# Two changed positions in the gate projection of a two-block transformer kernel: what the first copy of a head pair waits for, and where the second strip's gather stands on VectorE

## The reference, cut to what matters

```python
q, i_in, f_fw, f_bw, z = jnp.split(h @ w_in, 5, axis=-1)
for d, g in enumerate((f_fw, f_bw)):
    log_f = jnp.logaddexp(jnp.log(lbd), jnp.log1p(-lbd) + jax.nn.log_sigmoid(gf))
    k = (1.0 - lbd) * jax.nn.sigmoid(-gf)
...
o_l, _ = _hgrn2_bidir(q_l, v_l, gates_l, ctx_states)
...
o = _rmsnorm(o, o_gain).reshape(B, L, D_INNER).astype(z.dtype)
return (o * jax.nn.silu(z)) @ w_out
```

## Time and profile before

| | us |
|---|---|
| median of the runs | 2627.55 (2625.5 to 2629.52, 3 runs) |
| the profiled execution's own time | 2627.0 |
| its span in the trace | 2625.2 |
| PE busy | 2517.3 (96%) |
| DVE busy | 1199.5 (46%) |
| ACT busy | 605.6 (23%) |
| POOL busy | 258.0 (10%) |
| mean granted TensorE clock | 0.988 of full |

### The profile page before, as it was taken

The page is one execution under the profiler, slowest core; times in us unless marked ns, Lnnn a source line. Parts: engine busy times, 40 slices in busy tenths (PEclk is TensorE's granted clock), DMA queues, the critical chain, the costliest instruction groups (busy, mean ns, idle before and its releaser), DMA issues.

```text
span 2625.2 us, 33413 instructions
## 1 busy us (share of the span) xinstructions
PE 2517.3 (96%) x13400; PEld 1965.0 (75%) x13400; DVE 1199.5 (46%) x2083; ACT 605.6 (23%) x1202; POOL 258.0 (10%) x194
## 2 busy tenths in 40 slices
PE   7999999999999898899999999999999999999999
PEld 3687888878878576666786444678886587889998
DVE  2267585685775712254226111146665014115961
ACT  3132223232322112133224110021111013112211
POOL 0011111121111010000000000101210000003410
PEclk9999999999999998999999999999999999999999
DMA  9453343333424042212430122322333232254662
GB/s 352 157 177 128 112 144 112 133 144 117 149 96 145 2 143 77 79 40 56 125 97 17 48 80 64 97 64 82 96 102 89 66 80 65 81 178 135 170 174 68
DMA packets 320031, 284.83 MB, mean 108 GB/s; under 512 B 27650, under 2 KB 298634, under 8 KB 319546
## 3 DMA queue, kind: packets, MB, share of 16 engines
q1 hardware_dynamic: 318170, 279.08, 34.3%
q0 software_dynamic: 1280, 4.20, 0.4%
q10 hardware_dynamic: 479, 0.13, 0.0%
HBM read 280.24 MB, written 3.15 MB: 108 GB/s over the span
## 4 chain that ended last, share of the span: by engine, by line
PE 79%; DVE 12%; issue 7%; ACT 2%; DVEq 0%; POOL 0%; ACTq 0%; POOLq 0%
PE ps L1358 11%; PE ps L1287 9%; PE ps L721 9%; PE ps L1437 4%; PE ps L1425 4%; PE ps L781 4%; PE ps L1325 3%; PE ps L1299 3%; PE ps L819 3%; PE ps L905 2%; PE ps L976 2%; PE ps L925 2%; DVE arena L2316 2%; PE ps L1131 2%; PE ps L484 2%
## 5 line engine op out<-in xcount | busy, mean ns | idle before, releaser
L1287 PE MATMUL ps<-hT,ring_mem 128*128 128x512 f32 (+1 forms) x768 | 250.3, 486 | 0.0
L1287 PEld LDWEIGHTS ps<-hT,ring_mem 128*128 128x128 f32 x768 | 145.9, 190 | 101.3 <-issue 91.4
L721 PE MATMUL ps<-hT,ring_mem 128*128 128x256 f32 x672 | 164.2, 388 | 24.1 <-ACT arena L1592 16.3
L721 PE MATMUL ps<-xT,ring_mem 128*128 128x256 f32 x672 | 162.0, 384 | 7.2 <-DVE ring_mem L2013 7.2
L721 PEld LDWEIGHTS ps<-hT,ring_mem 128*128 128x128 f32 x672 | 127.7, 193 | 47.4 <-ACT arena L1592 19.1
L2247 DVE TENSOR_TENSOR arena<-ps,arena 128x512 f32<-128x512 f32 (+1 forms) x48 | 26.8, 558 | 291.3 <-PE ps L1299 291.3
L721 PEld LDWEIGHTS ps<-xT,ring_mem 128*128 128x128 f32 x672 | 129.6, 194 | 27.9 <-DVE ring_mem L2013 7.9
L1358 PE MATMUL ps<-hT,arena 128*128 128x256 f32 (+1 forms) x704 | 132.6, 333 | 6.9 <-ACT hT L505 6.9
L1358 PE MATMUL ps<-arena 128*128 128x256 f32 (+1 forms) x704 | 130.1, 328 | 0.0
L819 PE MATMUL ps<-arena,K_c 128*128 128x128 f32 x896 | 120.0, 288 | 8.5 <-ACT K_c L1629 8.4
L819 PEld LDWEIGHTS ps<-arena,K_c 128*128 128x128 f32 x896 | 116.4, 194 | 15.3 <-ACT K_c L1629 10.7
(11 more groups left out here) (307 smaller groups left out, 4324.0 us busy)
## 6 DMA issues: line engine op xcount, KB each, us to landing
ring_mem<-in_w_mod_dram SPq DMA_DIRECT2D x24, 2048.0 KB, 7.7
ring_mem<-in_w_up_dram SPq DMA_DIRECT2D x88, 512.0 KB, 5.2
ring_mem<-in_hg_w_in_dram SPq DMA_DIRECT2D x40, 1024.0 KB, 5.2
ring_mem<-in_w_in_dram SPq DMA_DIRECT2D x30, 1024.0 KB, 5.4
ring_mem<-in_w_down_dram SPq DMA_DIRECT2D x16, 1408.0 KB, 7.1
ring_mem<-in_ada_w_dram SPq DMA_DIRECT2D x8, 2048.0 KB, 7.7
ring_mem<-in_mla_w_in_dram SPq DMA_DIRECT2D x9, 1024.0 KB, 5.3
ring_mem<-in_hg_w_out_dram SPq DMA_DIRECT2D x8, 1024.0 KB, 12.1
```

Source lines behind the costliest of these rows:

```text
L721: mm = PE.matmul(dst, left[:, k, :], right[:, k, :], start=k == 0, stop=k == 3)
L1287: mm = PE.matmul(ps[:, j, 0:n], wj[:, k, m * 128:m * 128 + 128], hT[:, k, c0:T], start=k == 0, stop=k == 7)
```

## The change

Two edits. On ScalarE the copy of product one of a turn's first strip no longer waits for `unpacked` and `moved`, only for `o_full`; the copy of product two of the first strip now waits for these two. On VectorE, after term 3 of the scan, the gather of the second strip (`j` = 1, with the sums for the third) comes ahead of the read-out, where it came behind it. Terms 1, 5 and 7, at which other gathers stand, have no read-out.

```diff
@@ -1585,8 +1585,6 @@
             act.wait_ge(one_full, nth(i, j))
             if j == 0:
                 act.wait_ge(o_full, raised(i * 2 - 2))
-                act.wait_ge(unpacked, i)
-                act.wait_ge(moved, i)
             else:
                 act.wait_ge(whole_ready, nth(i, j - 1))
             S.activation(P1_hg, ps[:, 0, 0:256], ACT.Copy).then_inc(one_kept, 1)
@@ -1597,6 +1595,9 @@
 
         def hg_two_scalar(act, i, j):
             act.wait_ge(two_full, nth(i, j))
+            if j == 0:
+                act.wait_ge(unpacked, i)
+                act.wait_ge(moved, i)
             if j == 2:
                 act.wait_ge(lv_full, i * 16 - 14)
             S.activation(hg_part(j, 0, 256), ps[:, 0, 0:256], ACT.Copy).then_inc(two_kept, 1)
@@ -2407,10 +2408,10 @@
                     if not first and term == 2:
                         for hd in range(2):
                             hg_root_vector(dve, i - 1, hd)
+                    if gates and term % 2:
+                        hg_gather_vector(dve, st, i + 1, term // 2)
                     if not first and term == 3:
                         hg_read_vector(dve, st, i - 1)
-                    if gates and term % 2:
-                        hg_gather_vector(dve, st, i + 1, term // 2)
                     if gates and term == 4:
                         hg_mods_vector(dve, i + 1, 0)
                         for m in range(2):
```

## The result

| | before | changed |
|---|---|---|
| median, us | 2628.51 (4 runs) | 2599.82 (2596.28 to 2602.53, 4 runs) |
| ratio | | 0.9892, 95% interval 0.988 to 0.9904 |
| span of the profiled execution | 2625.2 | 2597.6 |
| PE busy | 2517.3 | 2508.6 |

The account below looks back on a forecast made before the run. PE was taken as the bound, busy 96% of the span. Gains of 20.9 us at the turn heads and 6.0 from the VectorE reordering, 26.9 together, gave a median of 2600.6 us, range 2594 to 2611.

Parts of the forecast that it names:

- What ended the wait at the head: Turn's head: PE's 2.63 us wait for the copy at 1592 ends with `unpacked`, not with `o_full` or the product.
- What is late next there: Turn's head: scores of term 1 wait for ScalarE's keys, starting at 9.63 instead of 11.99; 0.7 us of new waiting remains.
- The added wait at 1602: ScalarE's copy at 1602, now at 9.4 us, waits for `unpacked`, due at 5.7: costs nothing, 3.7 us in hand.
- the collision at the unpacking: GpSimd's 2510 of strip 0 lands beside VectorE's 1948 and 1951: bounds 0 and 1.07 us, taken as 0.
- The clock: Turn heads: about 5.4 us (four times 1.35) of the gain is clock coming back, if shorter waits leave it high.
- Edit two: VectorE after term 3, turns 2 to 7: 1.0 us per turn, 6.0 in all; ends 4.8 and 11.1.
- The tie between 2063 and GpSimd: Read-out's 2062 (now 2063) and GpSimd's 2510 start within 0.1 us; PE keeps 0.8, 1.3 or 1.85 us a turn.
- Rival A: Read-out beside GpSimd's sum: the collision is free, 1.85 us a turn, 32 in all, 2595.5 us; chance 0.18.
- Rival B: Term 5: the clock falls at the new waits of nearly 2 us, giving 2606 to 2610 us; chance 0.17.
- C: An unseen chain takes back most of the gain: about 9 us remain, 2618 us; chance 0.07.
- D: Turn's head: 1592 could be waiting for `o_full` or the product; no change, 2627 us; chance 0.03.
- E: Slower: low clock after the new waits at terms 1 and 5 in every turn, thirteen falls, up to 2642 us; chance 0.02.

Follow-up runs that it names:

- The written-out loop: ScalarE's loop over turns 1 to 6 written out instead of a Fori loop, against the changed kernel: 2597.35 us, ratio 0.9883.
- the kernel with the held sum: GpSimd's first sum of strip 2 waits until the products of term 4 are done, against the changed kernel: 2595.72 us, ratio 0.988.
- a kernel whose wait was 0.05 us longer: GpSimd's first sum of strip 2 waits until the read-out is done, against the changed kernel: 2609.83 us, one run.

## Why the prediction was right, point by point

- **What ended the wait at the head.** `unpacked` was last, as read from ScalarE's idle time: with both waits at the copy the head is 14.8 at clock 1.00, with only `moved` kept 13.2, with neither 12.4.
- **What is late next there.** 1596 plus 5.91 us gave 9.63 for the scores of term 1; they start at 9.56 (323.49 - 313.93). Head forecast 12.5, 11.8 and 11.7; measured 12.41, 11.71 and 11.59. The sum of the heads was forecast at 20.9 and measured at 21.4. The written-out loop showed that it was ScalarE's chain: a table load less, and the wait is gone.
- **The added wait at 1602 and the collision at the unpacking** cost nothing. The collision came at its full 1.07 us and was covered, within the bounds given.
- **The clock.** The 5.4 us came back: no head is below 1.00. A fall in turn 7 costs more than the 1.35 of the others: without one that head is 14.55 us in the kernel with edit two alone, against 16.24. The forecast of turn 7 does not hang on this.
- **Edit two.** Named were the four things that happened: PE 2.8 us ahead after the gather, a new wait of nearly 2 (1.79), 1970 back at 1.22, 2063 longer. The size was forecast at 6.0 and measured at 5.1. The tie between 2063 and GpSimd was taken in the middle (1.0 us a turn). In turns 2 to 6 GpSimd was ahead every time, by 0.03 to 0.05 us, and 2063 paid 1.0; in turn 7 VectorE won, and the gain there was 1.6. PE's 0.8 at the scores of term 5 shrinks by 0.1 in the scores themselves, which take 2.05 us behind the wait instead of 1.95. Taking the middle was a choice and not a reading; the rows of 1969 spoke for the full price.
- **Rival A** (no collision) is what the kernel with the held sum does: 1.7 us a turn instead of 0.7. **Rival B** (the clock falls at the new wait) did not come in the trace of the changed kernel and did in one of a kernel whose wait was 0.05 us longer, for 1.64 us in each of five turns. Its chance of 0.17 was no formality: five such falls would have made about 2608 of the 2599.8. That they stayed away is not explained by anything in the prediction, and in so far it was luck. **C, D and E** did not come. The thirteen falls of E are too many by the prediction's own waits, which are five at term 1 and six at term 5.
- **A premise of B that does not hold.** The prediction puts the new wait between 1.72 us, which the clock survived, and 2.63. The same trace of the kernel before has waits of 1.16 and 1.50 us, 2.6 us from one to the next, after which the clock was at 0.50:

```profile
1096.82 1.10 PE L431 MATMUL ps<-arena,ones 128*128 128x256 f32 x4 [1.16 <-ACT arena L400]
1099.42 2.05 PE L431 MATMUL ps<-arena,ones 128*128 128x512 f32 x2 [1.50 <-ACT arena L400]
```

```profile
1099.42:1101.42 2.00, 2.00 (x3) 0.97 (x4) 1.96 (x3) 0.00 (x0) 0.00 (x0) 0.50 0.00 0
```

So 1.72 us was no safe length.

- **Small misreadings.** The wait at the head of turn 2 was 2.46 us and not as long as the others. The part from line 484 on is 88.9 us in turns 2 to 7 and 85.9 in turn 1. Neither changes the sum.
- **How close it came** is partly chance. Over the turns the forecast was 26.9 and the measurement 26.5, with the heads 0.5 better and edit two 0.9 worse; another 1.0 us came from the part behind the turns, where nothing was changed.

## What to carry to other kernels

When a wait on several semaphores is split, look at which of them the engine's idle time names, and then follow the queue of the engine that waited to the next thing that TensorE needs from it: the gain ends there. An instruction moved ahead of another on a busy engine gives PE only what the displaced work does not take back one step later; ask also where the helper engine that it releases will now land. With GpSimd summing in SBUF, put instructions that read PSUM beside it.

## What was not expected of the hardware

- TensorE's clock fell behind waits of 1.84 us in five turns of 102.3 us each and in none of five turns of about 100 us with the same wait; behind waits of 2.5 to 2.6 us it fell in four turns of six and, in the kernel with edit two alone, in two of six; behind an unchanged wait of 2.41 us in three traces of 14. Two kernels that differ by 0.7 us a turn so came out 8 us apart in falls. Each ran once, so it is open whether the edit or the execution made that difference.
- In the loop over turns ScalarE loads an activation table (1.28 us) between roots and keys in every turn; with the loop written out that load was gone, and the one ahead of the roots stayed.
- With GpSimd ahead by 0.04 us, by the starts that the profile gives, VectorE's instruction with two SBUF inputs paid 1.0 us; with VectorE ahead by 0.24 it paid nothing, and the second one behind it 0.3.
